# Key projection on two column strips, scores on two PSUM banks, and the softmax finish moved into the next head's maxima

## The chip, the cores and the metric

The kernel runs on one core of a Trainium2 chip. The metric is the device time of one execution in microseconds; a kernel is run several times and the median counts.

## The reference

One inference step of a trunk with two layers, for 128 context tokens and 1024 latent tokens. The first layer is a long convolution beside latent attention, the second a Fourier mixer. Only the attention of the first layer matters here:

```python
q = (cq @ w_uq).reshape(B, L, N_HEADS_B, QK_DIM)            # 8 heads, 64 + 32 rotary
q = concat([q[..., :64], apply_axial_rope(q[..., 64:])])     # latent tokens only
kv = (keys_c @ w_ukv).reshape(B, Lk, N_HEADS_B, 64 + 64)     # Lk = 128 cached + 1024 latent
s = einsum('bqhd,bkhd->bhqk', q, k) * ATTN_SCALE
o = einsum('bhqk,bkhd->bqhd', softmax(s), v)
y = concat([y_a * silu(g_a), o * silu(g_b)]) @ w_out         # o is gated per element
```

Context tokens attend to their own 128 keys alone. In the kernel the context keys stand behind the 1152 keys of the latent tokens (ALLKEYS = 1280).

## The kernel before, in words

All engines run programs written out by hand and joined by semaphores; an engine takes its instructions in the order of the program. Attention is a pipeline over eight heads. In the function `attend(i, s)` each engine does its share of a head step: TensorE computes the scores and outputs of head s, projects keys and queries of head n = s + 1 and scores them once more to find each query's maximum, and finishes the row sums of head s - 1. Six of the eight steps stand in a loop of two.

Keys and queries are kept as a rounded part and a remainder (`k_hi`, `k_lo`, `q_hi`, `q_lo`), so that a score tile is three multiplies. TensorE's pieces in a step, in order: `scores(0)` (nine key tiles of 128, each in two halves of 512 queries), the last `outputs` of the head before, `project` of the key pieces k0 and k1 (384 keys each, 64 outputs, two multiplies of 128 rows), `row_sums` of the head before, k2, `scores(1)`, the query pieces q0, q1, q2 (384 columns each), and then for each tile from 2 on scores, outputs and, from tile 3 on, `max_scores` of the next head. k3 holds the last 128 keys and stands behind the outputs of tile 0. A float32 multiply is two passes in the trace.

PSUM has eight banks. Scores rotate over banks 0 to 2. Key and query pieces, then the maxima, rotate over banks 3 to 5 (`STEP_BANK`), so a piece waits until the one three before it has been read. Outputs gather in bank 6: the first half of the queries in rows 0 to 63, the second in 64 to 127, which is two column strips of TensorE. Row sums and the context tokens use bank 7.

ScalarE rounds the keys out of PSUM (L1278), copies queries (L1285), and makes the exponentials of each half tile (L1308). VectorE subtracts key remainders (`key_los`, L1661), rotates the queries (`queries`, L1645 to L1648: three operations a piece, the last with all operands in SBUF), finishes the head before (`finish`: reciprocal of the row sums L1703, two multiplies L1706, gate multiply L1710), and then goes through `maxima`: for each of eight query tiles two reduces (L1676 over banks 3 and 4, L1678 over bank 5), with query remainders (L1654) behind tiles 0, 2 and 4 and the values of the head (L1670) behind tile 5. TensorE's maximum passes of a tile wait for the reduces of the tile before. GpSimd adds up the exponentials, one add of 128 x 1024 for each tile from 1 on (L1904). At the end of `maxima` TensorE transposes the result, ScalarE negates it, and SP writes it as a row under the queries (L463); the next head's `scores(0)` waits for that. SP also loads weights two heads ahead (L455, L456) and, for each second head, the gate (L468), which waits for `finish` of the pair before.

In the trace PSUM is `bank`, the exponentials, their reciprocal and the values are in `SCR`, the added exponentials in `fw`, rounded keys in `WR_r`, key remainders in `KV_r`, weights and latents in `WR` and `KV`.

Of the kernel before, what the change touches and what calls it, by code (L numbers as in the profile page):

```python
# [56 lines left out]
STEPS = ("k0", "k1", "k2", "q0", "q1", "q2", "k3")  # L57
STEP_BANK = {name: 3 + n % 3 for n, name in enumerate(STEPS)}
KT9 = KEYS // P
# [11 lines left out]
def build(nc, T):  # L71
    ctx = ExitStack()
    with ctx:
# [244 lines left out]

        def ds1(x):
            return slice(x, x + 1) if isinstance(x, int) else bass.ds(x, 1)  # L320
# [37 lines left out]
        def _(sp):  # L358
# [92 lines left out]
            def w_load_next(i, s):  # L451

                sp.wait_ge(pj_mm, at(i, s, 7, 7))
# [75 lines left out]
        def _(pe):  # L529
# [264 lines left out]
            def project(i, s, *steps):  # L794

                m = s % 2
                for name in steps:
                    n, j = int(name[1]), STEPS.index(name)
                    if j == 0:
# [4 lines left out]
                    if j >= 3:  # L804
                        was, w = STEPS[j - 3]
                        pe.wait_ge(*((pj_k, at(i, s, 4, int(w) + 1)) if was == "k" else (pj_q, at(i, s, 3, int(w) + 1))))
                    wt, src, rows = (w_q[m], cqT, P) if name[0] == "q" else (w_k[m], keysT, NOPE)
                    a, w = KS3 * n, KS3 if n < 3 else P
                    product(bank[0:rows, STEP_BANK[name], 0:w], [(wt[:, k, 0:rows], src[:, k, a:a + w]) for k in range(2)]).then_inc(pj_mm, 1)

# [34 lines left out]
            def scores(i, s, kt):  # L845

                if kt == 0:
                    pe.wait_ge(pq_los, at(i, s, 3, 3))
                    pe.wait_ge(mx_in, at(i, s, 32, 32))
                for half in range(2):  # L850
                    j = 2 * kt + half
                    pe.wait_ge(st_exp, at(i, s, UNITS, unit(*divmod(j - 3, 2)) + 5 if j >= 3 else unit(*divmod(j + 15, 2)) + 5 - UNITS))
                    shifted_scores(s, bank[:, j % 3, :], slice(kt * P, (kt + 1) * P), slice(512 * half, 512 * (half + 1)))

            def prompt_scores(i, s):
                if s:
                    pe.wait_ge(o_cp, at(i, s, 3, -1))
                shifted_scores(s, bank[:, 7, 0:P], slice(KEYS, ALLKEYS), slice(LS, TOK))

            def prompt_outputs(i, s):  # L860
                pe.wait_ge(st_exp, at(i, s, UNITS, 2 * KT9 - 1 + 4))
                nc.tensor.matmul(bank[0:VD, 7, P:2 * P], v_head[s % 2][:, 9, :], pT_prompt, start=True, stop=True)
                nc.tensor.matmul(bank[0:VD, 7, 2 * P:3 * P], ones[:, 0:VD], pT_prompt, start=True, stop=True).then_inc(pp_mm, 1)

            def outputs(i, s, kt):

                pe.wait_ge(st_exp, at(i, s, UNITS, unit(kt, 1) + 5))
                if kt == 0:
                    pe.wait_ge(kv_set, at(i, s, 1, 3))
                    if s:  # L870
                        pe.wait_ge(o_cp, at(i, s, 3, -1))
                for half in range(2):
                    last = nc.tensor.matmul(bank[VD * half:VD * (half + 1), 6, :], v_head[s % 2][:, kt, :], pT[kt % 3][:, 512 * half:512 * (half + 1)],  # L873
# [3 lines left out]
            def row_sums(i, s):  # L877
# [3 lines left out]
                for half in range(2):  # L881
                    last = nc.tensor.matmul(bank[VD * half:VD * (half + 1), 7, :], ones[:, 0:VD], p_acc[:, 512 * half:512 * (half + 1)], start=True, stop=True)
                last.then_inc(sum_mm, 1)

            def attend(i, s, before=True, after=True):
# [5 lines left out]
                if after:  # L891
                    project(i, n, "k0", "k1")
                if before:
                    row_sums(i, s - 1)
                if after:
                    project(i, n, "k2")
# [3 lines left out]
                for kt in range(2, KT9):  # L900
# [8 lines left out]
                    if after:  # L909
                        if kt == 2:  # L910
                            project(i, n, "k3")
# [131 lines left out]
        def _(act):  # L1043
# [229 lines left out]
            def keys(i, s, *parts):  # L1273
                for n in parts:
                    name = f"k{n}"
                    act.wait_ge(pj_mm, at(i, s, 7, 1 + STEPS.index(name)))
                    a, w = KS3 * n, KS3 if n < 3 else P
                    nc.scalar.copy(k_hi[s % 2][0:NOPE, a:a + w], bank[0:NOPE, STEP_BANK[name], 0:w]).then_inc(pk_his, 1)  # L1278

            def query_rows(i, s, *parts):  # L1280

                for n in parts:
                    name = f"q{n}"
                    act.wait_ge(pj_mm, at(i, s, 7, 1 + STEPS.index(name)))
# [16 lines left out]
            def exps(i, s, kt):  # L1301

                for half in range(2):
# [4 lines left out]
                    nc.scalar.activation(pT[kt % 3][:, 512 * half:512 * (half + 1)], bank[:, (2 * kt + half) % 3, :], ACT.Exp, scale=SCALE).then_inc(st_exp, 1)  # L1308
# [714 lines left out]
```

## Time and profile before

| | us |
|---|---|
| median of 3 runs | 1526.43 (1524.68 to 1526.88) |
| the profiled execution | 1525.2 |
| its span (first to last instruction) | 1523.1 |
| TensorE busy, whole span | 1395.9 (92%) |
| VectorE busy | 694.1 (46%) |
| GpSimd busy | 216.7 (14%) |
| attention, first scores to last finish | 631.9 to 987.3 |

Times inside the kernel are counted from the span's start. A stretch is cut out of the span and shows each engine's busy time and the clock that TensorE was granted in it, as a share of full speed (1.00 is 2.4 GHz, 0.50 is 1.2 GHz). A timeline row gives start, duration, engine, line, what is written and read, and in brackets how long the engine was idle before it and what ended that.

### The profile page before, as it was taken

Reading aid. Unit: us, or ns where it says so; the run is one execution under the profiler, and the core shown is the slowest. Engines: PE = TensorE matmul, PEld = TensorE weight load, DVE = VectorE, ACT = ScalarE, POOL = GpSimd, SP = SyncE. Lnnn points to the kernel's source line nnn. Section 1 sums busy time; section 2 is a strip of 40 time slices with the busy share of each in tenths; the row PEclk is TensorE's granted clock in tenths of the full one; section 3 lists DMA queues with packets and bytes.
Section 4 is the critical chain, followed back from the end, with each engine's and each line's share of the span. In section 5 each row is a group of like instructions: output and inputs, shape, how many; then the busy total and the mean of one; then the engine's idle time right before and its main releaser. Section 6 shows DMA issues by size and latency. Waiting matters only on the chain.

```text
span 1523.1 us, 17427 instructions
## 1 busy us (share of the span) xinstructions
PE 1395.9 (92%) x6698; PEld 1069.7 (70%) x6698; DVE 694.1 (46%) x938; ACT 412.7 (27%) x737; POOL 216.7 (14%) x163
## 2 busy tenths in 40 slices
PE   6598999999999988699888998799999999999897
PEld 2497999999923446345444545388889999998786
DVE  5611423232243896577776667455422222223643
ACT  2722211121122022233333322345431111111321
POOL 2310000000032000044443444400000000000000
PEclk8799999999989999699899998899999999999999
DMA  8300333333320024100000000022220000002411
GB/s 366 124 1 32 138 119 113 125 139 106 127 100 11 28 90 155 39 6 6 21 5 21 0 0 16 15 102 83 90 82 30 29 29 29 29 29 100 167 52 56
DMA packets 29917, 107.00 MB, mean 70 GB/s; under 512 B 3659, under 2 KB 7951, under 8 KB 26416
## 3 DMA queue, kind: packets, MB, share of 16 engines
q1 hardware_dynamic: 28144, 99.30, 18.1%
q10 hardware_dynamic: 1728, 7.08, 1.2%
q8 instruction: 30, 0.49, 0.1%
q14 instruction: 15, 0.12, 0.0%
HBM read 89.67 MB, written 16.66 MB: 70 GB/s over the span
## 4 chain that ended last, share of the span: by engine, by line
PE 76%; DVE 12%; issue 5%; DMA 3%; ACT 1%; SPq 1%; POOL 1%; DVEq 0%; PEld 0%; POOLq 0%; ACTq 0%; PEldq 0%
PE bank L533 42%; PE bank L956 13%; PE bank L842 6%; PE bank L873 4%; PE bank L828 2%; PE bank L748 2%; PE bank L1023 2%; DVE SCR L1703 2%; DMA SCR<-x_sample_in 2%; DVE amax_part L1676 2%; PE bank L684 1%; PE bank L544 1%; PE bank L692 1%; SPq L368 1%; DMA H<-w_oo_in 1%
## 5 line engine op out<-in xcount | busy, mean ns | idle before, releaser
L533 PE MATMUL bank<-H_r,WR_r 128*128 128x384 f32 x1728 | 352.8, 336 | 1.6 <-DVE H_r L1798 1.2
L533 PEld LDWEIGHTS bank<-H_r,WR_r 128*128 128x128 f32 x1728 | 302.6, 188 | 6.4 <-issue 4.2
L533 PE MATMUL bank<-H_r,SCR_r 128*128 128x384 f32 x480 | 161.0, 335 | 0.0
L1904 POOL TENSOR_TENSOR fw<-fw,SCR 128x1024 f32<-128x1024 f32 x56 | 132.9, 2373 | 128.2 <-ACT SCR L1308 125.4
L1308 ACT ACTIVATE SCR<-bank 128x512 f32<-128x512 f32 x144 | 83.8, 597 | 148.3 <-PE bank L842 118.2
L533 PE MATMUL bank<-KV,WR 128*64 128x384 f32 (+3 forms) x288 | 106.0, 512 | 18.0 <-DVE KV_r L1661 13.7
L1868 POOL TENSOR_SCALAR ssq<-ssq 128x1 f32<-128x1 f32 (+1 forms) x36 | 16.1, 446 | 624.1 <-ACT bank L1051 523.1
L956 PE MATMUL bank<-H_r,WR_r 128*128 128x512 f32 x432 | 100.8, 396 | 3.9 <-DVE SCR L1831 3.9
L533 PE MATMUL bank<-H_r,WX_r 128*128 128x384 f32 x384 | 99.8, 341 | 3.3 <-PEq L624 3.3
L956 PE MATMUL bank<-KV_r 128*128 128x512 f32 x288 | 92.4, 398 | 9.2 <-DVE SCR_r L1746 9.2
L533 PEld LDWEIGHTS bank<-KV,WR 128*128 128x128 f32 (+1 forms) x288 | 48.1, 172 | 75.0 <-issue 47.8
L956 PEld LDWEIGHTS bank<-H_r,WR_r 128*128 128x128 f32 x432 | 82.9, 192 | 21.6 <-DVE SCR L1831 4.1
L1472 DVE SCALAR_TENSOR_TENSOR SCR<-bank,col,SCR 128x766 f32<-128x766 f32 (+1 forms) x96 | 43.0, 510 | 107.3 <-ACT SCR L1191 105.9
L533 PEld LDWEIGHTS bank<-H_r,SCR_r 128*128 128x128 f32 x480 | 90.5, 189 | 0.0
L873 PE MATMUL bank<-SCR 128*64 128x512 f32 x288 | 83.1, 648 | 2.0 <-DVE H L1706 2.0
L533 PEld LDWEIGHTS bank<-H_r,WX_r 128*128 128x128 f32 x384 | 69.6, 190 | 5.4 <-PEq L624 3.7
L1802 DVE TENSOR_TENSOR WR_r<-WR,WR_r 128x1024 fp32r<-128x1024 f32 x16 | 19.6, 1225 | 113.4 <-ACT WR_r L1083 113.4
L956 PEld LDWEIGHTS bank<-KV_r 128*128 128x128 f32 x288 | 55.1, 191 | 21.5 <-issue 10.0
L1676 DVE TENSOR_REDUCE amax_part<-bank 128x1 f32<-128x768 f32 x64 | 60.9, 951 | 18.4 <-PE bank L828 18.4
L533 PE MATMUL bank<-KV 128*128 128x258 f32 (+1 forms) x288 | 61.3, 372 | 4.6 <-DVE KV L1818 4.6
L842 PE MATMUL bank<-SCR_r,WR_r 96*128 96x512 f32 (+1 forms) x152 | 64.0, 421 | 0.0
L533 PEld LDWEIGHTS bank<-KV 128*128 128x128 f32 x288 | 52.7, 190 | 14.9 <-ACT KV L1365 5.9
(277 smaller groups left out, 2069.8 us busy)
## 6 DMA issues: line engine op xcount, KB each, us to landing
WR<-w_mod_in SPq DMA_DIRECT2D x16, 1024.0 KB, 6.9
SCR<-w_in_in SPq DMA_DIRECT2D x20, 512.0 KB, 3.4
H<-w_mod_in SPq DMA_DIRECT2D x4, 2048.0 KB, 14.7
SCR<-x_sample_in SPq DMA_DIRECT2D x16, 512.0 KB, 15.1
WR<-w_io_in SPq DMA_DIRECT2D x16, 512.0 KB, 3.4
sp_rows<-SCR SPq DMA_DIRECT2D x9, 512.0 KB, 2.6
KV<-sp_rows SPq DMA_DIRECT2D x9, 512.0 KB, 8.8
H<-w_oe_in SPq DMA_DIRECT2D x2, 2048.0 KB, 13.0
```

Source lines behind the costliest of these rows:

```text
L533: last = nc.tensor.matmul(out, l, r, start=(n == 0), stop=(n == len(pairs) - 1))
L748: last = nc.tensor.matmul(bank[:, b0 + r // 2, r % 2 * 256:(r % 2 + 1) * 256], zz[kt][:, zz_at[r][q], c * P:(c + 1) * P], ti[kt][:, r, q, ...
L828: last = nc.tensor.matmul(bank[:, 3 + n, 0:KS3], q, k_hi[m][0:QK, KS3 * n:KS3 * (n + 1)], start=True, stop=True)
L842: last = nc.tensor.matmul(out, l, r, start=(n == 0), stop=(n == 2))
L873: last = nc.tensor.matmul(bank[VD * half:VD * (half + 1), 6, :], v_head[s % 2][:, kt, :], pT[kt % 3][:, 512 * half:512 * (half + 1)], star ...
L956: last = nc.tensor.matmul(bank[:, 2 * (t % 2) + j, :], y_sl[l][t % 2][a][:, k, :], w[l][k][:, j * 512:(j + 1) * 512], start=(k == 0 and a ...
L1023: last = nc.tensor.matmul(bank[:, 6 + n % 2, m_ * 256:(m_ + 1) * 256], lhs, csw[:, :], start=True, stop=True)
L1308: nc.scalar.activation(pT[kt % 3][:, 512 * half:512 * (half + 1)], bank[:, (2 * kt + half) % 3, :], ACT.Exp, scale=SCALE).then_inc(st_exp, 1)
L1472: add = lambda o, i: stt(o, i, w, o, ALU.mult, ALU.add)
L1676: nc.vector.tensor_reduce(amax_part[:, 2 * t:2 * t + 1], bank[:, 3:5, 0:KS3], mybir.AxisListType.XY, ALU.max).then_inc(mx_red, 1)
L1703: link(nc.vector.reciprocal(rinv, bank[:, 7, :]))
L1904: ptt(p_acc, pT[0] if kt == 1 else p_acc, pT[kt % 3], ALU.add).then_inc(p_added, 1)
```

## The change

- The keys are projected in two steps, kA and kB, of 640 keys each. The first 320 go to rows 0 to 63 of a bank, the other 320 to rows 64 to 127: two column strips, in alternation. k3 is gone. ScalarE and VectorE take the keys in four pieces of 320.
- kA, kB and q0 have banks 3, 4 and 5; q1 waits for two pieces of key remainders, q2 for all four. The weights' load waits for the fifth step instead of the seventh.
- Scores use banks 0 and 1, one for each half, and wait for the exponential of the same half of the tile before. Row sums and context tokens go to bank 2. Outputs alternate between banks 6 and 7 from head to head, and no longer wait for the finish.
- `finish` is cut in three: reciprocal, the two multiplies, the gate multiply. They stand behind tiles 1, 3 and 6 of the next head's maxima instead of between the second and the third piece of key remainders. In the last step, which has no next head, they stand alone.

```diff
-STEPS = ("k0", "k1", "k2", "q0", "q1", "q2", "k3")
+STEPS = ("kA", "kB", "q0", "q1", "q2")
 STEP_BANK = {name: 3 + n % 3 for n, name in enumerate(STEPS)}
+KS4 = ALLKEYS // 4
...
+        def key_bank(n):
+            return bank[NOPE * (n % 2):NOPE * (n % 2 + 1), 3 + n // 2, 0:KS4]
...
 # TensorE, project
-                    if j >= 3:
-                        was, w = STEPS[j - 3]
-                        pe.wait_ge(*((pj_k, at(i, s, 4, int(w) + 1)) if was == "k" else (pj_q, at(i, s, 3, int(w) + 1))))
-                    wt, src, rows = (w_q[m], cqT, P) if name[0] == "q" else (w_k[m], keysT, NOPE)
-                    a, w = KS3 * n, KS3 if n < 3 else P
-                    product(bank[0:rows, STEP_BANK[name], 0:w], [(wt[:, k, 0:rows], src[:, k, a:a + w]) for k in range(2)]).then_inc(pj_mm, 1)
+                    if name in ("q1", "q2"):
+                        pe.wait_ge(pj_k, at(i, s, 4, 2 * int(name[1])))
+                    if name[0] == "q":
+                        a = KS3 * int(name[1])
+                        last = product(bank[:, STEP_BANK[name], 0:KS3], [(w_q[m][:, k, :], cqT[:, k, a:a + KS3]) for k in range(2)])
+                    else:
+                        a = 2 * KS4 * (name == "kB")
+                        for k in range(2):
+                            for h in range(2):
+                                last = nc.tensor.matmul(bank[NOPE * h:NOPE * (h + 1), STEP_BANK[name], 0:KS4], w_k[m][:, k, 0:NOPE],
+                                                        keysT[:, k, a + KS4 * h:a + KS4 * (h + 1)], start=(k == 0), stop=(k == 1))
+                    last.then_inc(pj_mm, 1)
...
 # TensorE, scores
-                    j = 2 * kt + half
-                    pe.wait_ge(st_exp, at(i, s, UNITS, unit(*divmod(j - 3, 2)) + 5 if j >= 3 else unit(*divmod(j + 15, 2)) + 5 - UNITS))
-                    shifted_scores(s, bank[:, j % 3, :], slice(kt * P, (kt + 1) * P), slice(512 * half, 512 * (half + 1)))
+                    pe.wait_ge(st_exp, at(i, s, UNITS, unit(kt - 1, half) + 5 if kt else unit(KT9 - 1, half) + 5 - UNITS))
+                    shifted_scores(s, bank[:, half, :], slice(kt * P, (kt + 1) * P), slice(512 * half, 512 * (half + 1)))
...
 # TensorE, outputs
-                    if s:
-                        pe.wait_ge(o_cp, at(i, s, 3, -1))
-                    last = nc.tensor.matmul(bank[VD * half:VD * (half + 1), 6, :], v_head[s % 2][:, kt, :], pT[kt % 3][:, 512 * half:512 * (half + 1)],
+                    last = nc.tensor.matmul(bank[VD * half:VD * (half + 1), 6 + s % 2, :], v_head[s % 2][:, kt, :], pT[kt % 3][:, 512 * half:512 * (half + 1)],
...
 # TensorE, attend
-                    project(i, n, "k0", "k1")
+                    project(i, n, "kA")
...
-                    project(i, n, "k2")
+                    project(i, n, "kB")
...
-                        if kt == 2:
-                            project(i, n, "k3")
...
 # VectorE, maxima
+                    if before and t in (1, 3, 6):
+                        finish(i, s - 2, (t + 1) // 3)
...
 # VectorE, attend
-                    key_los(i, n, 0, 1)
-                if before:
-                    finish(i, s - 1)
-                if after:
-                    key_los(i, n, 2)
+                    key_los(i, n, 0, 1, 2, 3)
                     queries(i, n, 0, 1, 2)
-                    key_los(i, n, 3)
-                    maxima(i, n)
+                    maxima(i, n, before)
+                elif before:
+                    for part in range(3):
+                        finish(i, s - 1, part)
```

TensorE in step 1, behind the first score tile and up to the second. `L873` are outputs, `L533` with 64 rows key pieces, `L882` row sums; ISA and REGISTER_ALU rows are waits. Before:

```order
L873 MATMUL bank<-SCR 64x512 x2
L800 ISA
L802 ISA
L803 ISA
L533 MATMUL bank<-KV,WR 64x384 x4
L879 ISA
L880 REGISTER_ALU
L882 MATMUL bank<-fw_75,ones 64x512 x2
L533 MATMUL bank<-KV,WR 64x384 x2
```

After, where `L880` are the outputs, `L817` key pieces and `L889` row sums:

```order
L880 MATMUL bank<-SCR 64x512 x2
L804 ISA
L806 ISA
L807 ISA
L817 MATMUL bank<-KV,WR 64x320 x4
L886 ISA
L887 REGISTER_ALU
L889 MATMUL bank<-fw_75,ones 64x512 x2
L817 MATMUL bank<-KV,WR 64x320 x4
```

Six key multiplies of 384 columns have become eight of 320, four on each side of the row sums.

VectorE in the same step, from the second piece of key remainders to the queries (`L1661` remainders, `L1703` reciprocal, `L1706` multiplies, `L1710` gate, `L1645` and on queries). Before:

```order
L1661 TENSOR_TENSOR KV_r<-bank,WR_r 64x384
L1703 RECIPROCAL SCR<-bank 128x512
L354 REGISTER_ALU
L1706 ISA
L1706 TENSOR_TENSOR H<-bank,SCR 64x512
L1706 ISA
L1706 TENSOR_TENSOR H<-bank,SCR 64x512
L1708 REGISTER_ALU
L1710 TENSOR_TENSOR H<-H,SCR 64x1024
L1659 REGISTER_ALU
L1661 TENSOR_TENSOR KV_r<-bank,WR_r 64x384
```

After, in the maxima (`L1675` and `L1677` are the two reduces of a tile, `L1653` query remainders), from the first reduce of tile 1 on:

```order
L1675 TENSOR_REDUCE amax_part<-bank 128x1
L1676 REGISTER_ALU
L1677 TENSOR_REDUCE amax_part<-bank 128x1
L1705 RECIPROCAL SCR<-bank 128x512
L359 REGISTER_ALU
L1674 REGISTER_ALU
L1675 TENSOR_REDUCE amax_part<-bank 128x1
L1676 REGISTER_ALU
L1677 TENSOR_REDUCE amax_part<-bank 128x1
L1653 TENSOR_TENSOR SCR_r<-SCR,WR_r 96x384
```

The reciprocal has left the stretch ahead of the queries and stands between the reduces of tiles 1 and 2; the multiplies and the gate multiply follow behind tiles 3 and 6.

## Rows read from the trace of the kernel before

**Rows 1.** The page's part 1: busy time, share and instructions of each engine.
```profile
PE 1395.9 (92%) x6698; PEld 1069.7 (70%) x6698; DVE 694.1 (46%) x938; ACT 412.7 (27%) x737; POOL 216.7 (14%) x163
```

**Rows 2.** Stretches (from:to, length, busy time of each engine, granted clock): three head steps.
```profile
671.88:714.18 42.30, 38.23 (x157) 21.19 (x156) 30.89 (x44) 15.04 (x30) 18.85 (x9) 1.00 0.02 6
...
714.18:762.92 48.74, 43.15 (x156) 23.98 (x156) 33.07 (x45) 15.37 (x31) 18.94 (x9) 0.89 0.05 17
...
950.97:987.34 36.37, 28.30 (x110) 14.01 (x109) 16.75 (x14) 10.92 (x19) 19.89 (x9) 0.92 0.00 0
```

**Rows 3.** Timeline (start, duration, engine, line, operation): a slow step's front.
```profile
714.17 0.50 PE L842 MATMUL bank<-WR_r 97*128 97x512 f32 x1
...
716.69 2.42 PE L533 MATMUL bank<-KV,WR 128*64 128x384 f32 x7
...
718.63 0.64 PE L882 MATMUL bank<-fw,ones 128*64 128x512 f32 x1
...
718.94 0.49 PE L533 MATMUL bank<-KV,WR 128*64 128x384 f32 x1
...
720.45 3.34 DVE L1703 RECIPROCAL SCR<-bank 128x512 f32<-128x512 f32 x1
...
723.01 2.74 PE L533 MATMUL bank<-KV,WR 128*128 128x384 f32 x8
...
725.36 2.04 DVE L1710 TENSOR_TENSOR H<-H,SCR 64x1024 f32 x1
...
728.01 0.56 DVE L1645 TENSOR_TENSOR SCR<-bank,rope_q 32x384 f32<-32x384 f32 x1
...
728.04 2.20 PE L533 MATMUL bank<-KV,WR 128*128 128x384 f32 x4 [2.28 <-DVE KV_r L1661]
...
733.02 0.42 DVE L1648 TENSOR_TENSOR SCR<-SCR,WR 32x256 f32<-32x256 f32 x1
...
733.96 0.50 PE L842 MATMUL bank<-WR_r 97*128 97x512 f32 x1
...
735.47 0.68 PE L828 MATMUL bank<-WR_r,WX_r 96*128 96x384 f32 x3
...
736.42 2.39 POOL L1904 TENSOR_TENSOR fw<-fw,SCR 128x1024 f32<-128x1024 f32 x1 [0.65 <-ACT SCR L1308]
```

**Rows 4.** Stretches at the lower clock, PEclk as share of full speed.
```profile
728.81:732.22 3.41, 3.41 (x9) 2.28 (x7) 2.94 (x7) 0.99 (x2) 0.00 (x0) 0.50 0.40 153
...
752.70:759.53 6.83, 6.83 (x20) 4.35 (x19) 1.91 (x5) 1.74 (x4) 2.34 (x1) 0.50 0.00 0
...
612.80:636.65 23.85, 14.81 (x32) 8.66 (x33) 12.57 (x21) 2.75 (x4) 0.00 (x0) 0.50 0.03 8
```

**Rows 5.** Timeline: the maxima of a quick step, then of a slow one.
```profile
693.35 0.96 DVE L1676 TENSOR_REDUCE amax_part<-bank 128x1 f32<-128x768 f32 x1 [0.86 <-PE bank L828]
...
701.83 0.96 DVE L1676 TENSOR_REDUCE amax_part<-bank 128x1 f32<-128x768 f32 x1 [0.25 <-PE bank L828]
...
709.36 0.17 DVE L1686 TENSOR_REDUCE amax<-amax_part 128x8 f32<-128x16 f32 x1
...
736.01 0.96 DVE L1676 TENSOR_REDUCE amax_part<-bank 128x1 f32<-128x768 f32 x1 [1.37 <-PE bank L828]
...
737.35 1.87 DVE L1654 TENSOR_TENSOR SCR_r<-SCR,WX_r 96x384 fp32r<-96x384 f32 x1
...
756.49 0.17 DVE L1686 TENSOR_REDUCE amax<-amax_part 128x8 f32<-128x16 f32 x1
```

**Rows 6.** One line's instructions: ns min/median/max of the queries' last operation.
```profile
L1648 DVE TENSOR_TENSOR SCR<-SCR,WR x24: 416/550/2154, 606.7 to 921.2; 32x384 f32<-32x384 f32 x16, 32x256 f32<-32x256 f32 x8
```

**Rows 7.** Timeline: the last head step, where outputs wait for the finish.
```profile
957.94 1.39 DVE L1706 TENSOR_TENSOR H<-bank,SCR 64x512 f32<-64x512 f32 x2
...
959.48 1.08 PE L873 MATMUL bank<-SCR 128*64 128x512 f32 x4 [1.98 <-DVE H L1706]
```

**Rows 8.** The gate load's line: time from issue to landing.
```profile
DMA to landing us min/median/max: 3.7/3.7/3.8
```

## What the change was predicted to do

> **What bounds the kernel now.** TensorE is busy for 92% of the span [rows 1], but that is a mean over stages, so I cut the attention stage into its eight head steps, each from the first score pass of a head to that of the next [rows 2]. The change touches nothing outside this stage and the projection of the first head ahead of it (three rows stand for eight steps: a quick one, a slow one and the last). Steps 1 to 6 are alike in the code and last 950.97 - 671.88 = 279.09 us together: two take 42.30 us (granted clock 1.00), the other four 48.6 on average (0.89 in the row). So there are quick and slow steps, and the difference is partly the clock.
>
> Read next the front of a slow step in order of time [rows 3]. From the first score pass (714.17) to the first pass of the next head's maxima (735.47) go 21.30 us. In it TensorE waits 2.28 us by the row, and stands still from about 725.59 to 728.04, for the third part of the key remainders on VectorE, which is queued behind the row sums' reciprocal (3.34), two multiplies (1.39 [rows 7]) and the gate multiply (2.04). Then the granted clock falls to 0.50 from 728.81 to 732.22 [rows 4], and the four query passes that start at 728.04 last 2.20 us.
>
> After the front VectorE sets the pace: it reduces two pieces of scores per token tile, eight times, with other work between. First reduce to end of the maxima: 16.18 us in a quick step (693.35 to 709.53), 20.65 in a slow one (736.01 to 756.66) [rows 5]. Two things make it slow: a VectorE operation whose operands are all in SBUF ends only once GpSimd's running add has ended (the query remainder at 737.35 ends at 739.22, 0.41 after the add of 736.42 to 738.81 [rows 3]), and a later collision of the kind lets TensorE pause, and the clock is at 0.50 from 752.70 to 759.53 [rows 4]. The tail, from the end of the maxima to the next head's first score pass, is 714.17 - 709.53 = 4.64 in a quick step and 762.92 - 756.66 = 6.26 in a slow one [rows 2, 5].
>
> **The front after the change,** in us from the first score pass, at full clock. Scores and the last outputs' passes: 2.52 (714.17 to 716.69). Query passes of 384 columns start every (2.74 - 0.48) / 7 = 0.323; one of 320 should take 0.323 x 320/384 = 0.269. The keys have 16 of these on two strips. That strips run side by side is in the rows: four 512-column output passes on two strips take 1.08 together [rows 7], where by the spacing above four in a row would start 0.43 apart and take over 1.7. So I count eight slots, 2.15. (Before: 12 x 0.323 = 3.87, and about 4 x 0.108 = 0.43 for the last 128 columns further on.) Row sums 0.90, like the outputs; the change to full width 0.1. The second score tile starts at 2.52 + 2.15 + 0.90 + 0.1 = 5.7 (before: 723.01 - 714.17 - 1.51 = 7.33), takes 1.51 like the tile from 733.96 to 735.47, then twelve query passes 3.87 to 11.1, scores 1.4, outputs 1.0, scores 1.5: first maximum pass at 15.0, if only TensorE counted.
>
> Two waits could be late instead. The query banks now wait for four pieces of key remainders: ScalarE copies and VectorE subtracts 320 columns in about 0.5 each (VectorE takes 0.56 over 384 in the row at 728.01), so the last is ready about 7.2, before the third query product at 9.8: no wait. The other is VectorE's rotary work on the queries: 5.01 us from its first operation to the start of its last (728.01 to 733.02), so from 8.7 to 13.7. That last operation has all operands in SBUF; it and its like took 0.416 at best and 2.154 at worst [rows 6]. GpSimd's add starts some 2.4 after its score tile does (733.96 to 736.42), so the one of the third tile at 13.5. The add is first by 0.2 us: the operation ends near 13.5 + 2.37 + 0.29 = 16.2. Bounds of the first maximum pass are 15.0 and 16.2; I take 16.2, and the first reduce 0.55 later, at **16.7**. Before it was 21.47 in the quick step and 21.84 in the slow one (693.35 - 671.88, 736.01 - 714.17).
>
> **The maxima after the change.** VectorE now carries the three parts of the finish inside this chain: 3.34 + 0.15 after the first two tiles, 1.39 after the fourth, and the gate multiply, 1.1 free or 2.04 behind GpSimd: 5.9 to 6.9, I take 6.4. They fill three gaps in which VectorE waits for TensorE between two tiles (0.25 in the row at 701.83, where nothing stands between two tiles; the others are a little longer): -1.0. So 16.18 + 6.4 - 1.0 = 21.6 where GpSimd collides as in a quick step. Nothing hides the 6.4; in the old place it was partly under query and score passes, and that cover is given up.
>
> While the reciprocal runs, TensorE has one maximum and one output group left, 1.5 us, and then waits for the next reduce: 3.34 + 0.15 + 0.95 - 1.5 = a pause of 2.9. The pause of 2.45 in the front of the slow step was followed by a low clock, so I expect one here in nearly every step. Its price: 6.8 us at half clock leave TensorE 3.4 us behind; for two tiles TensorE needs 1.4 + 0.9 + 1.0 = 3.3 at full and 6.6 at half clock, VectorE by my estimate 5.3 (four reduces, about 3, and a remainder or a part of the finish): 1.3 late. Bounds 0 (VectorE still last) and 3.4; I take 1.3, and **22.9** for the stage. A second pause follows near the end, when tile 7's reduce waits for the gate multiply, of 1.3 to 1.8 us: at the edge of what brought the clock down. A low clock there costs what it costs a slow step from its eighth score tile on, about 2.9 us.
>
> A step is then 16.7 + 22.9 + 4.64 = **44.2**, between 42.9 (no drop) and 47.1 (both). Against a quick step that is a loss of 1.9, against a slow one a gain of 4.4.
>
> **The rest.** Scores on two PSUM banks instead of three: a score half waits for the exponential of the half two before it. Both exponentials of a tile were done, and the add released, 2.4 us after its first score pass (733.96 to 736.42); with the output passes between them tiles start 2.3 or more apart, and a half waits only for the matching half. So nothing in steps 0 to 6, and at most 0.5 where two tiles stand back to back in step 7. Outputs alternating between two banks remove the wait of step 7 (1.98, then VectorE's multiply [rows 7]) and the pause before its low clock: -2 to -4, I take -3. Lead-in and step 0 have no finish work to move; each saves the keys' 3.87 + 0.43 - 2.15 = 2.15; I take -2.3 each, the head of the stage being at half clock in part. On SP the gate load waits for the finish, which now comes at 37 of a step instead of 13; behind it in the queue are two weight loads (needed two steps later, so free) and the row of maxima that the next scores wait for. The finish is done some 3.3 us before that row is, the load lands 3.7 after issue [rows 8]: 0 to 2 us in each of three steps; I take 0.
>
> **The sum.** Six steps: 6 x 44.2 = 265.2, second drops in two of them 5.8, against 279.1: -8.1. With -2.3, -2.3 and -3: -15.7. The profiled execution took 1525.2, 1.2 below the median of the runs shown, so 1509.5 in a like execution and **1511** as a median.
>
> **Rivals.** *Second drop in all six:* 17.4 for 5.8, 1523; for it speaks that the pause near the end is bound by the reduces, against it that it is shorter than any that brought a drop. *No drops at all:* 42.9 a step, less 7.6 elsewhere, 1497; against it stands the 2.9 us pause. *Slower:* the clock falls at the reciprocal and does not rise before the step's end. Where TensorE was busy 14.81 of 23.85 us at half clock in the lead-in, it stayed low all that time [rows 4]. From tile 3's maximum to the next head some 13 us of passes are left; at half clock 26, so a step of 50.4, 302.4 for six, and 1542. It decides from a step of 47.8 (279.1 + 7.6 over six). Against it: both kinds of drop in the slow steps ended within 6.83 us. *The strips do not run side by side:* 2.15 us more in eight places, 1528; the output passes of rows 7 speak against it.
>
> In rows 3 a row-sum pass (718.63) starts before a key pass that stands ahead of it in the program (718.94). So passes of different strips overtake. The Trainium skill (TensorE: Matmul & The Clock Gate, "Part 3: Packing small matmuls — row/col tiling") says that matmuls start and end strictly in program order. By that rule each multiply's second pass would hold up the other strip, five slots instead of four per key product: 0.54 per step, 4.3 in all, 1515. The row differs, and I follow the row; its chance is 0.05.
>
> **How the numbers follow.** Forecast (1511) 0.51; second drop everywhere (1523) 0.17; no drop (1497) 0.13; strict program order (1515) 0.05; strips serial (1528) 0.04; clock stays low (1542) 0.10. A measurement of this kernel can tell about 0.2%, 3 us. Faster by more: 0.51 + 0.13 + 0.05 + most of 0.17, 0.11 = 0.80; within: 0.06 + 0.03 = 0.09; slower: 0.01 + 0.10 = 0.11. The range leaves out the slow rivals and the lower half of "no drop": 1499 to 1524.
>
> **What would show it.** Right: steps of about 44 us, few at 42 or 48; no wait of the third query product on key remainders; key passes in pairs 0.27 apart; a TensorE pause near 3 us behind the reciprocal, then a clock of 0.50. Wrong: full clock through the maxima (then 1497), or 0.50 up to the next head (then over 1526), or a wait for the row of maxima's DMA before the first scores.

## The result, and the profile after

| | before | after |
|---|---|---|
| median, us | 1526.66 (1524.68 to 1528.48, 4 runs) | **1516.17** (1514.42 to 1518.55, 4 runs) |
| profiled execution; its span | 1525.2; 1523.1 | 1517.42; 1515.3 |
| granted clock over the span | 0.95 | 0.94 |

The ratio is 0.9933, 95% interval 0.9912 to 0.9953. Forecast: 1511, range 1499 to 1524, chance of a gain 0.80. On another chip the same pair gave 1512.56 to 1532.34, ratio 0.9877 (0.9850 to 0.9903), so the two chips put the gain at 10 and at 20 us.

The engines' shares of the span are as before. TensorE is busy 8.0 us less, and the span is 7.8 us shorter, but where that was won does not show in the page's part 1, against [rows 1]:

```profile
PE 1387.9 (92%) x6698; PEld 1068.1 (70%) x6698; DVE 691.4 (46%) x938; ACT 412.7 (27%) x737; POOL 216.6 (14%) x163
```

It shows by steps. The same stretches as in [rows 2], from a head's first score pass to the next head's (from:to, length, busy time of PE, PEld, DVE, ACT, POOL, granted clock), steps 1 to 6 and the last:

```profile
674.99:720.83 45.84, 40.52 (x156) 22.62 (x156) 31.24 (x44) 15.18 (x30) 18.75 (x9) 0.89 0.02 5
720.83:764.99 44.16, 38.74 (x156) 22.00 (x156) 31.92 (x45) 15.29 (x31) 18.84 (x9) 0.92 0.06 18
764.99:809.10 44.11, 38.78 (x157) 22.01 (x156) 31.50 (x44) 15.18 (x30) 18.86 (x9) 0.92 0.01 5
809.10:858.14 49.04, 42.43 (x157) 23.21 (x156) 33.19 (x46) 15.39 (x31) 19.76 (x9) 0.86 0.05 16
858.14:901.79 43.65, 38.58 (x156) 21.93 (x156) 30.80 (x43) 15.19 (x30) 17.93 (x8) 0.92 0.00 0
901.79:945.93 44.14, 38.69 (x156) 22.00 (x156) 31.91 (x45) 15.28 (x31) 18.85 (x9) 0.92 0.04 13
945.93:979.80 33.87, 26.95 (x110) 13.25 (x109) 17.61 (x14) 10.93 (x20) 20.68 (x9) 0.96 0.00 0
```

There are no quick steps of 42.3 and slow ones of 48.6 any more: four of six take 43.65 to 44.16, and none has a clock of 1.00. The front of the second of them (720.83), in order of time; the columns are those of [rows 3]:

```profile
723.34 1.25 PE L817 MATMUL bank<-KV,WR 128*64 128x320 f32 x8
724.41 1.03 PE L889 MATMUL bank<-fw,ones 128*64 128x512 f32 x4
725.27 1.25 PE L817 MATMUL bank<-KV,WR 128*64 128x320 f32 x8
726.45 0.50 PE L852 MATMUL bank<-WR_r 97*128 97x512 f32 x1
...
734.18 2.37 POOL L1906 TENSOR_TENSOR fw<-fw,SCR 128x1024 f32<-128x1024 f32 x1 [2.92 <-ACT SCR L1311]
734.87 1.97 DVE L1647 TENSOR_TENSOR SCR<-SCR,WR 32x256 f32<-32x256 f32 x1
...
736.97 0.79 PE L838 MATMUL bank<-WR_r,WX_r 96*128 96x384 f32 x3 [0.97 <-DVE SCR L1647]
737.62 0.96 DVE L1675 TENSOR_REDUCE amax_part<-bank 128x1 f32<-128x768 f32 x1 [0.78 <-PE bank L838]
```

Eight key passes (L817) take 1.25 us, and the next work starts 1.07 after the first of them: four slots of 0.27, with one pass on each strip in a slot. The second score tile starts at 5.62 of the step. No query pass waits for key remainders. The queries' last rotary operation (L1647) is caught behind GpSimd's add and ends 0.29 after it, and the first reduce comes at 16.79. Its maxima, and then two stretches at the lower clock, behind the reciprocal of this step and at the end of the step from 809.10:

```profile
740.88 3.34 DVE L1705 RECIPROCAL SCR<-bank 128x512 f32<-128x512 f32 x1
...
745.36 1.33 PE L838 MATMUL bank<-WR_r,WX_r 96*128 96x384 f32 x3 [2.88 <-DVE amax_part L1675]
...
746.48 0.63 PE L852 MATMUL bank<-WR_r 97*128 97x512 f32 x1
...
749.92 0.96 DVE L1675 TENSOR_REDUCE amax_part<-bank 128x1 f32<-128x768 f32 x1 [0.67 <-PE bank L838]
...
754.99 2.37 POOL L1906 TENSOR_TENSOR fw<-fw,SCR 128x1024 f32<-128x1024 f32 x1 [2.62 <-ACT SCR L1311]
...
756.04 2.40 DVE L1714 TENSOR_TENSOR H<-H,SCR 64x1024 f32 x1
...
760.17 0.17 DVE L1687 TENSOR_REDUCE amax<-amax_part 128x8 f32<-128x16 f32 x1
```

```profile
745.33:752.16 6.83, 6.80 (x17) 4.21 (x18) 5.91 (x9) 1.19 (x2) 2.12 (x1) 0.52 0.01 1
...
847.45:857.69 10.24, 9.98 (x29) 4.67 (x27) 2.42 (x5) 2.76 (x6) 4.68 (x2) 0.50 0.26 79
```

While the reciprocal runs TensorE stands for 2.88 us, and then runs at half clock: a first score pass takes 0.63 instead of 0.50. Such a pause and a drop behind it stand in all six steps. A second stretch at 0.50, near the end, stands in two: 3.41 us in the first, 10.24 in the fourth.

### The profile page after: what moved, and what is told of

It is laid out like the page before. It is cut to its first block, busy times and chain, and to the rows that moved or that the text cites. A ratio compares the mean times of both kernels' runs of the same rounds, so it can differ in the third digit from the quotient of the medians.

```text
span 1515.3 us, 17391 instructions
## 1 busy us (share of the span) xinstructions
PE 1387.9 (92%) x6698; PEld 1068.1 (70%) x6698; DVE 691.4 (46%) x938; ACT 412.7 (27%) x737; POOL 216.6 (14%) x163
## 4 chain that ended last, share of the span: by engine, by line
PE 76%; DVE 12%; issue 4%; DMA 3%; POOL 2%; ACT 1%; SPq 0%; DVEq 0%; PEld 0%; POOLq 0%; ACTq 0%; PEldq 0%
PE bank L538 40%; PE bank L961 13%; PE bank L852 4%; PE bank L880 3%; PE bank L838 2%; PE bank L753 2%; PE bank L1028 2%; DMA SCR<-x_sample_in 2%; DVE amax_part L1675 2%; DVE SCR L1705 2%; DVE SCR L1647 1%; PE bank L817 1%; POOL fw L1906 1%; PE bank L689 1%; PE bank L549 1%
## 5 line engine op out<-in xcount | busy, mean ns | idle before, releaser
L880 PE MATMUL bank<-SCR 128*64 128x512 f32 x288 | 86.1, 669 | 0.0
L1675 DVE TENSOR_REDUCE amax_part<-bank 128x1 f32<-128x768 f32 x64 | 61.0, 953 | 16.3 <-PE bank L838 15.3
L1888 POOL TENSOR_TENSOR H<-SCR 128x512 f32<-128x512 f32 x9 | 15.8, 1754 | 319.8 <-DVE SCR L1529 303.5
L538 PE MATMUL bank<-KV,WR 128*128 128x384 f32 (+1 forms) x160 | 60.7, 531 | 0.0
```

Of the source, the lines that this page charges most:

```text
L538: last = nc.tensor.matmul(out, l, r, start=(n == 0), stop=(n == len(pairs) - 1))
L880: last = nc.tensor.matmul(bank[VD * half:VD * (half + 1), 6 + s % 2, :], v_head[s % 2][:, kt, :], pT[kt % 3][:, 512 * half:512 * (half + 1 ...
L1675: nc.vector.tensor_reduce(amax_part[:, 2 * t:2 * t + 1], bank[:, 3:5, 0:KS3], mybir.AxisListType.XY, ALU.max).then_inc(mx_red, 1)
```

## The experiments

The theory: the gain is the keys' eight slots and the outputs' second bank; moving the finish trades a loss at full clock against clock drops; its reciprocal is not hidden, makes the pause, and the pause brings the drop. The main rival: the move is the gain. All edits are made to the changed kernel. Where a step is given, it is from the profiled execution; ratios are to the kernel before on the same chip.

**undo_move** puts the whole finish back ahead of the queries.

```diff
-                    if before and t in (1, 3, 6):
-                        finish(i, s - 2, (t + 1) // 3)
...
-                    key_los(i, n, 0, 1, 2, 3)
+                    key_los(i, n, 0, 1)
+                    if before:
+                        for part in range(3):
+                            finish(i, s - 1, part)
+                    key_los(i, n, 2, 3)
```

> The finish stands again between the second and the third piece of key remainders; strips and banks stay as changed. Theory (the gain comes from the shorter key passes and from VectorE having less between them; the move itself is about neutral): the row sums end near 4.6 us of a step, reciprocal, multiplies and gate multiply take 3.34 + 1.39 + 2.04, so the last key remainder is done near 12.6, the third query product waits about 2.8 us for it, and the first reduce comes at 19 to 20.5 instead of 16.8. The maxima then hold no finish: 16.2 to 17.5 us. A step of 40 to 43 without a late clock drop, 46 with one. Six steps 250 to 275 against 270.9; a total of 1500 to 1520, no more than 10 us from the changed kernel either way. Rival (the move of the reciprocal is what gained): steps of 42.3 and 48.7 as in the kernel before, total 1524 to 1527.

1510.30 (1492.31 to 1514.73), ratio 0.9886 (0.9852 to 0.9921). Two of its steps, the usual one and the one with drops, and the front of the first in order of time:

```profile
709.14:749.81 40.67, 36.16 (x157) 20.08 (x156) 30.41 (x45) 15.15 (x31) 18.93 (x9) 1.00 0.06 20
831.08:879.39 48.31, 42.28 (x156) 23.13 (x155) 32.33 (x44) 15.30 (x30) 18.92 (x9) 0.86 0.00 0
```

```profile
719.37 1.28 DVE L1712 TENSOR_TENSOR H<-H,SCR 64x1024 f32 x1
720.68 1.01 DVE L1660 TENSOR_TENSOR KV_r<-bank,WR_r 64x320 fp32r<-64x320 f32 x2
...
721.74 1.56 PE L538 MATMUL bank<-KV,WR 128*128 128x384 f32 x4 [2.73 <-DVE KV_r L1660]
...
728.93 0.96 DVE L1675 TENSOR_REDUCE amax_part<-bank 128x1 f32<-128x768 f32 x1 [0.78 <-PE bank L838]
```

The third query product waits 2.73 us, the first reduce comes at 19.80, and five steps of six take 40.65 at full clock. So keys and banks alone shorten a quick step by 1.65 (42.30 before), and the move of the finish then costs 3.5 (44.15, which holds a clock drop). To compare the two directly, both ran again side by side, **after_again** (the changed kernel) and **undo_again**:

> The changed kernel once more, beside undo_again on one chip. By the steps of its profile (one drop of the clock in every step, a second in some: 44.1 to 49.0) it should lie at 1509 to 1518.

> undo_move once more, beside the changed kernel. Theory (the move of the finish gains nothing: a step with it undone is 40.65 us at full clock and 48.3 with two drops, against 44.1 for the changed kernel, and only the number of steps with drops decides): each step with drops costs 7.7, so times lie at 1490 plus 0 to 5 of these, and the median within 8 us of the changed kernel on either side. Rival (the move is worth its 4 us a step against the slow steps that the kernel before has): 1516 to 1526, at least 5 us over the changed kernel.

1512.56 (1509.45 to 1518.61) and 1512.91 (1499.98 to 1521.23); ratios 0.9877 (0.9850 to 0.9903) and 0.9877 (0.9856 to 0.9898). In time the move of the finish is worth nothing that these runs can tell (each ratio is good to 3 or 4 us); the rival falls, and the gain is that of keys and banks. With the move undone a step without a drop is 3.5 shorter, but the times scatter by 21 us, those of the changed kernel by 9: the move makes the steps more alike. (The profiled executions of undo_move and undo_again were the fastest of their runs; one step with drops costs 7.7 us, so the others may have had two or three more of them. That is argued, not seen: a later arrival at the attention, taken up below, can be part of it.)

**recip_early** moves the reciprocal alone.

```diff
-                    if before and t in (1, 3, 6):
+                    if before and t in (3, 6):
...
-                    key_los(i, n, 0, 1, 2, 3)
+                    key_los(i, n, 0, 1)
+                    if before:
+                        finish(i, s - 1, 0)
+                    key_los(i, n, 2, 3)
```

> Only the reciprocal goes back in front of the queries, between the second and the third piece of key remainders; multiplies and gate multiply stay in the maxima. Theory (the 3.3 us in the maxima are not hidden and cause the 2.9 us pause and the first clock drop): VectorE has room for 3.34 us between the row sums (4.6) and the first query piece (8.4 to 8.7), so the first reduce stays at 16.8 to 17.3; the stage loses 3.5 and, without the pause, the drop's 1.3: a step of 39.5 to 40.5, seven steps 4 to 4.8 each, total 1484 to 1492. If the key remainders come late and the query passes pause, half of that: 1500. Rival (TensorE sets the pace, VectorE's work in the maxima is covered): no change, 1513 to 1519.

1495.62 (1492.93 to 1503.83), ratio 0.9786 (0.9740 to 0.9833). A step without and one with a drop, and the first reduce of the first:

```profile
712.36:753.20 40.84, 36.51 (x157) 20.02 (x156) 31.36 (x45) 15.24 (x31) 18.92 (x9) 1.00 0.06 20
753.20:796.87 43.67, 39.62 (x156) 21.42 (x155) 31.06 (x44) 15.19 (x30) 19.46 (x9) 0.92 0.02 5
```

```profile
729.39 0.96 DVE L1675 TENSOR_REDUCE amax_part<-bank 128x1 f32<-128x768 f32 x1 [0.78 <-PE bank L838]
```

The first reduce comes at 17.03, only 0.24 later: nearly all of the reciprocal lies in time in which VectorE had waited there. The drop at +24 is gone, but five of six steps have one from +27 to +37, four of them behind TensorE's other pause (1.44 to 1.58, at the gate multiply); the step without a drop has that pause, too. The theory was right in kind; the time lies 4 us above its range, and those drops are what it had not counted.

**short_recip** tests pause and drop in place.

```diff
-                    link(nc.vector.reciprocal(rinv, bank[:, 2, :]))
+                    link(nc.vector.reciprocal(rinv[:, 0:64], bank[:, 2, 0:64]))
```

> The changed kernel with the reciprocal taken over 64 of its 512 columns only (seven eighths of it are left out). Theory (the pause of 2.9 us that TensorE makes behind the reciprocal brings the clock drop at +24 us of each step): the reciprocal takes about 0.45 instead of 3.34, the pause falls under 0.5 us, and the drop at +24 is gone from all six steps; first reduce unchanged at 16.8, stage 18 to 18.5 instead of 22.5, a step of 40 to 40.5 where no late drop comes, 42 to 44 where one does (the pause of 1.5 us behind the gate multiply stays). 1488 to 1500. Rival (the drop at +24 comes whatever the pause, as 2.75 us of pause at +10 brought none in five of six steps of undo_move): VectorE's 2.9 us are saved, but 0.50 stands in a stretch near +24 in most steps: 41.3 and more, 1497 to 1505.

1491.10 (1485.30 to 1495.18), ratio 0.9752 (0.9715 to 0.9789). Two steps, without and with a late drop, and the reciprocal in the timeline of the first:

```profile
797.95:838.57 40.62, 36.47 (x156) 20.12 (x155) 29.19 (x45) 15.26 (x31) 18.90 (x9) 1.00 0.06 19
838.57:880.48 41.91, 37.98 (x156) 20.71 (x155) 28.79 (x44) 15.15 (x30) 18.90 (x9) 0.96 0.00 0
```

```profile
818.01 0.54 DVE L1705 RECIPROCAL SCR<-bank 128x64 f32<-128x64 f32 x1
```

The reciprocal takes 0.54, the pause of 2.88 is gone, and so is the drop at +24, in all six steps: theory, not rival. Five of the six have a later drop, from +27 to +37. A step without any drop is 3.54 shorter than the changed kernel's usual one. 2.80 of that is the reciprocal itself, so the drop behind it costs 0.7 to 0.8 (VectorE's idle time in the maxima falls by 0.8). So the long reciprocal brings that drop. That the length of the pause alone does it is not shown: undo_move's pause of 2.73 brought none in five of six steps.

**keys_twice** and **keys_by_strip** take up the strips.

```diff
-                        for k in range(2):
+                        for k in (0, 1, 0, 1):
```

> Every pass of the key projection runs twice (the second time over the same sums, so the keys are not the reference's): 8 products of 320 columns more a step, which is the TensorE time of keys on one strip after the other. Theory (TensorE sets the front of a step): the second score tile starts 2.15 us later, at 7.8 instead of 5.6, the first reduce at 18.9 instead of 16.8, eight projections cost 8 x 2.15 = 17 us: 1531 to 1535 by the scale of 1516, ratio to the changed kernel 1.010 to 1.012. Rival (the front is set by ScalarE and VectorE, or by GpSimd's adds): second tile later, but first reduce within 0.5 of 16.8, and no more than 4 us in all.

1527.58 (1523.60 to 1535.68), ratio 1.0015 (0.9982 to 1.0049). (The second round starts the sums anew, so the keys stay what they were.) In the step from 719.38:

```profile
721.88 2.32 PE L817 MATMUL bank<-KV,WR 128*64 128x320 f32 x16
...
727.15 0.50 PE L852 MATMUL bank<-WR_r 97*128 97x512 f32 x1
...
738.33 0.96 DVE L1675 TENSOR_REDUCE amax_part<-bank 128x1 f32<-128x768 f32 x1 [0.78 <-PE bank L838]
```

The second score tile starts at 7.77, the first reduce is at 18.95 in each step, 2.16 later. So a microsecond of key passes is a microsecond of the front, and the whole gain over the kernel before is gone with it. By the quotient of the ratios it costs 0.8% against the first result and 1.4% against after_again, on either side of the forecast; four steps have a late drop, where the changed kernel's profile has two.

```diff
-                        for k in range(2):
-                            for h in range(2):
+                        for h in range(2):
+                            for k in range(2):
```

> The four products of a key step are issued strip by strip (both products of rows 0 to 63, then both of rows 64 to 127) instead of alternating. Theory (passes of different strips overtake one another, as the rows before the change show): the two strips still run side by side as far as the passes can be looked ahead; second score tile within 0.4 us of 5.6, total within 4 us of the changed kernel. Rival (passes start strictly in program order, so that only neighbours on different strips overlap): of eight passes in a row only the middle two overlap, seven slots of 0.269 instead of four, 0.8 us for each of two key steps: second tile at 7.2, first reduce at 18.4, eight heads 11 to 13 us.

1509.33 (1508.44 to 1515.19), ratio 0.9890 (0.9860 to 0.9921), that is, no change.

```profile
719.66 1.30 PE L817 MATMUL bank<-KV,WR 128*64 128x320 f32 x8
720.74 1.08 PE L889 MATMUL bank<-fw,ones 128*64 128x512 f32 x4
```

Eight passes take 1.30 instead of 1.25: still four slots, although the four passes of one strip are issued ahead of the four of the other. The row sums start 1.08 after the first of them; by seven slots it would be over 1.8. So a pass starts ahead of earlier ones on the other strip. The Trainium skill (TensorE: Matmul & The Clock Gate, "Part 3: Packing small matmuls — row/col tiling") has matmuls start and end in program order; the row speaks against it for two column strips.

**rot_psum** takes the queries' last rotary operation away from GpSimd.

```diff
-                    link(tt_(rtmp[64:96, 0:w], bank[96:128, b, 0:w], rope_q[96:128, a:a + w], ALU.mult))
+                    link(tt_(bank[96:128, b, 0:w], bank[96:128, b, 0:w], rope_q[96:128, a:a + w], ALU.mult))
...
-                    tt_(q[64:96, a:a + w], q[64:96, a:a + w], rtmp[64:96, 0:w], ALU.add).then_inc(pj_q, 1)
+                    tt_(q[64:96, a:a + w], bank[96:128, b, 0:w], q[64:96, a:a + w], ALU.add).then_inc(pj_q, 1)
```

> The queries' second rotary product is written into PSUM instead of SBUF, so that the last rotary operation has one operand in PSUM. Theory (that operation waits for the end of GpSimd's add because all its operands are in SBUF, 1.97 us for 0.42 to 0.55): it takes about 0.5 to 0.6, ends 1.3 to 1.5 us earlier, the first reduce comes at 15.3 to 15.6 instead of 16.8, bounded below by the passes (15.0 + 0.55); a step 1.2 shorter, eight heads 8 to 10 us: 1506 to 1509. Rival (the passes bound the first reduce, or the wait for GpSimd only moves on to the next operation with all operands in SBUF, the query remainder behind tile 0): no more than 2 us, 1514 to 1517.

1519.27 (1516.27 to 1522.68), ratio 0.9927 (0.9898 to 0.9956): no gain over the changed kernel. The step from 725.09, in order of time:

```profile
738.44 2.39 POOL L1906 TENSOR_TENSOR fw<-fw,SCR 128x1024 f32<-128x1024 f32 x1 [2.92 <-ACT SCR L1311]
...
738.79 0.43 DVE L1647 TENSOR_TENSOR SCR<-bank,SCR 32x256 f32<-32x256 f32 x1
...
740.64 0.96 DVE L1675 TENSOR_REDUCE amax_part<-bank 128x1 f32<-128x768 f32 x1 [1.42 <-PE bank L838]
...
741.04 2.37 POOL L1906 TENSOR_TENSOR fw<-fw,SCR 128x1024 f32<-128x1024 f32 x1 [0.22 <-ACT SCR L1311]
...
742.09 1.74 DVE L1653 TENSOR_TENSOR SCR_r<-SCR,WX_r 96x384 fp32r<-96x384 f32 x1
```

The operation takes 0.43 under a running add, and the first reduce comes at 15.55 as forecast. But VectorE then meets the next add with the query remainder (L1653), which has both inputs in SBUF and ends 0.42 after that add: 1.74 instead of 0.55, 1.19 of the 1.24 won. The rival named this operation. The Trainium skill (SBUF — State Buffer, "Who interferes with whom") says that a VectorE instruction with two SBUF inputs contends with a GpSimd one that reads SBUF, and one with at most one such input, outside the modes that use both ports, doesn't; both rows agree.

**combo** joins recip_early and rot_psum and puts the gate multiply behind tile 7. **combo2** is combo with the rotary product in PSUM only from the third head on; **combo2_again** ran it beside **recip_gate**, which has the early reciprocal and the late gate multiply and leaves the rotary product in SBUF.

```diff
-                    if before and t in (1, 3, 6):
-                        finish(i, s - 2, (t + 1) // 3)
+                    if before and t in (3, 7):
+                        finish(i, s - 2, t // 3)
...
 # combo2, on top of combo's rotary product
+                    part = bank[96:128, b, 0:w] if s >= 2 else rtmp[64:96, 0:w]
```

> The reciprocal early as in recip_early, the rotary product through PSUM as in rot_psum, and the gate multiply behind tile 7 instead of tile 6. Theory: the two gains add (4 to 4.8 and 1.2 a step), since one lies in the maxima and the other in front of them, and the second pause (tile 7's reduce waiting for the gate multiply) goes: a step of 38 to 39.5, total 1474 to 1486. Rival (with VectorE relieved TensorE's passes set the pace; a step of passes alone is 36 to 38 us, by TensorE's busy time of 38.2 in the quick step less 2.15): gains add only in part, 1486 to 1495.

> As combo, but the rotary product goes through PSUM only for the heads projected in steps 1 to 6; the lead-in and step 0, where combo lost the collision's gain again (its query remainder took the wait, step 0 43.6 us with a drop, against 38.7 to 39.0 with the old form), keep it in SBUF. Theory: steps 1 to 6 as in combo (38 to 39), step 0 at 39: 3 to 5 us less than combo, 1472 to 1480. Rival (step 0's drop in combo came by chance of that run): no difference beyond 2 us.

> recip_early with the gate multiply behind tile 7 instead of tile 6; the rotary product stays in SBUF. Theory (the gate multiply behind tile 6 runs into GpSimd's add and holds up tile 7, 1.5 us of pause and the late drops; behind tile 7 it has the end of the step): first reduce 17.0 as in recip_early, gate multiply 1.2 instead of 2.4, no pause over 1.2 us and no late drop: a step of 39 to 40 in all six, 6 to 14 us under recip_early: 1477 to 1488 by the scale of 1532 for the kernel before. Rival (the late drops come from the collision at the rotary's last operation, which combo2 also removed): drops stay in three or more steps, 1488 to 1496.

> combo2 once more, beside recip_gate: 1468 to 1477; what it gains over recip_gate is the rotary product through PSUM, which ends the front 0.9 us earlier (first reduce 16.1 against 17.0), 5 to 6 us in six steps if the maxima keep their length.

combo 1480.09 (1476.14 to 1484.71), ratio 0.9666 (0.9629 to 0.9703); **combo2 1471.57** (1470.03 to 1476.76), **0.9642** (0.9613 to 0.9671), and again 1473.07, 0.9646 (0.9619 to 0.9673); recip_gate 1488.13 (1482.25 to 1491.76), 0.9723 (0.9693 to 0.9754). Two steps of combo2, then two of recip_gate with the gate multiply of the second:

```profile
668.45:706.55 38.10, 36.69 (x157) 20.16 (x156) 28.98 (x44) 15.04 (x30) 18.88 (x9) 1.00 0.02 6
706.55:745.24 38.69, 36.80 (x156) 20.14 (x156) 29.56 (x45) 15.14 (x31) 19.32 (x9) 1.00 0.06 21
```

```profile
676.43:715.45 39.02, 36.38 (x156) 20.18 (x155) 29.77 (x44) 15.04 (x30) 18.89 (x9) 1.00 0.02 6
715.45:758.00 42.55, 39.34 (x157) 22.02 (x156) 30.54 (x45) 15.19 (x31) 19.37 (x9) 0.92 0.06 19
```

```profile
751.98 1.22 DVE L1714 TENSOR_TENSOR H<-H,SCR 64x1024 f32 x1
```

combo lies in its theory's range. In combo2 TensorE is busy 36.7 of 38.1 us, and no step from 1 to 6 has a drop. In recip_gate the gate multiply takes 1.22 and steps without a drop are 39.0 to 39.9, as forecast, but two of six still drop: its time lies between theory and rival. So the rotary product through PSUM, worth nothing by itself, is worth something once the reciprocal is out of the maxima: 0.9 a step in front, and the two drops. The medians differ by 15 us (1473.07 for combo2_again, 1488.13). Not all of it need be the rotary product: of the 20.0 us between the profiled executions 11.8 lie in the head steps, and 6.5 are a later arrival at the attention, which the edit does not touch. combo's step 0 took 43.56 with a drop behind its maxima (rot_psum's 43.49), combo2's 37.35 and 38.90 without: by the steps that theory held; the two ratios alone, 0.9666 and 0.9642, do not tell combo from combo2.

## Where the prediction was right and wrong

- **The sum** came to -15.7; measured are -10.5 by the medians and -19.8 on the second chip.
- **Front**: second tile 5.62 (forecast 5.7), first reduce 16.79 (16.7), bound by GpSimd's add as taken (without that wait it came at 15.55, rot_psum). **Maxima**: 22.72 (22.9). **Tail**: 4.65 (4.64). **Step**: 44.16 (44.2); six steps 270.9 (271.0), with the second drop in two, as counted. That it would be two and not none or six was a guess.
- **Terms of the maxima were off and made up for each other**, so that 22.72 came so near is in part luck. The gate multiply met the add and took 2.40, over the 1.1 to 2.04 given, so the finish was 7.25 (with 0.12 behind the reciprocal) and not 6.4. The drop behind the reciprocal cost 0.8 and not 1.3: VectorE waited 0.67 us once for it. The query remainders, taken as in a quick step, met the adds less: 2.5 us in the step from 764.99, where the quick step from 671.88 had 3.2. The late drops were mis-sized, too: 1.7 and 4.9 us, where 2.9 each was counted.
- **Against a quick step a loss of 1.9, against a slow one a gain of 4.4**: 44.16 - 42.30 = 1.86 and about 4.5. undo_move shows what that loss is made of: 1.65 won by keys and banks, 3.5 lost by the move.
- **Last step** -2.5 (36.37 to 33.87; forecast -3): TensorE no longer waits for the multiplies [rows 7], and the clock drop that stood behind that wait is gone. This is read from the trace; no run takes the outputs' second bank away alone.
- **Lead-in and step 0**, -2.3 each: -1.1 and -1.26. The size was right at like clock. In undo_move, whose lead-in falls to half clock as that of before does, they are -2.05 (first key split to first scores, 33.98 to 31.93) and -2.64 (39.99 to 37.35). In the profiled execution of after two stretches at half clock there were 3.4 us longer each, and took it back. Step 0 of the same code took 38.7 in after_again and recip_gate, 37.33 in undo_again and 37.35 in combo2.
- **The rest of the miss** is not in the change's stages. Those give -1.1 - 1.26 - 8.15 - 2.5 = -13.0, the span -7.8. The difference is about the 5.5 us by which the profiled execution reached the attention later, in code that is the same (granted clock from 0 to 590 us 0.94, before 0.95). Runs whose code is the same up to there come in two groups: the first score pass stands at 636.3 to 637.9 us in after, after_again, rot_psum, combo and recip_gate, and at 631.1 to 631.5 in undo_move, undo_again, recip_early, short_recip, combo2 and combo2_again. The kernel before was profiled once (631.9), but its times on the other chips fall into two groups as well, most at 1524 to 1528 or 1530 to 1533, and its four on the first chip are all in the lower one. So the late arrival is probably not the change's doing, and part of why the two chips give 10 and 20 us; no late trace of the kernel before exists to show it.
- **Rivals**: "no drops" did not come, as each step had one, nor did the second drop in all six. The strips run side by side and out of order (keys_by_strip), and strips in series would have cost the whole gain (keys_twice). In the six steps the clock came back within 10.24 us of each drop, so "stays low" did not come. The gate's load kept no score pass waiting (tail 4.65). Scores on two banks cost next to nothing, as taken: two tiles back to back in the last step start 1.65 apart instead of 1.50.
- **What it did not see**: the place of the reciprocal was judged for the whole finish only. In the front VectorE has room for its 3.34 us (recip_early, first reduce 17.03), not for the finish's 6 (undo_move, 19.80).

## What to carry over

Cut a moved block into its parts and price each place apart: here the reciprocal belonged in VectorE's wait for the keys, the gate multiply at the very end, and putting both into the reduce chain cost more than the shorter key passes had won on a quick step. Where VectorE and GpSimd collide on SBUF operands, freeing one operation can hand the wait to the next one like it, as in rot_psum, so see first which operation meets the next add. And compare steps at the same clock before you put a gain down to an edit.

## What was not expected of the hardware

- **A pause alone does not settle the clock.** 2.88 us at +21.6 brought a drop in every step (after, after_again, rot_psum: 18 of 18), and so it did in keys_twice, at +23.8, and keys_by_strip. 2.75 at +9.9 brought one in 3 of 12 (undo_move, undo_again), 2.28 in 4 of 6 before. And recip_gate, with no pause over 0.98 but three of 0.8 to 0.98 in each step (at +15.4, +24.0 and +26.8), had 2 of 6; combo2, with one such pause in each step (at +25.8) and none over 0.96, 0 of 12 (in two runs). What decides it is open.
- **Two strips overtake each other over four passes**: issued strip by strip they still ran in pairs, eight in 1.30 us against 1.25.
- **A reciprocal over 64 columns takes 0.54 us, one over 512 3.34.**
